# Padding the tiles of xT and the slots of the split weights so that they stand at different offsets within 512 bytes

## The reference, cut to what matters

```python
qkv = h @ w_qkv                                   # 2048 x 6144
x = x + y @ w_o                                   # 2048 x 2048
x = x + (silu(conv(h @ w_gate)) * (h @ w_up)) @ w_down        # width 5632
...
c_q, c_kv, k_rope, q_d, k_d, v_d, q_idx, k_idx, w_idx = split(h @ w_in)
x = x + concat([mla(...), dsa(...)]) @ w_out
x = x + cross_attention(h, mem)
x = x + square(relu(h @ w_up)) @ w_down           # width 8192
return rmsnorm(x, g_final)
```

## Time and profile before

| | |
|---|---|
| median of 2 runs | 2344.15 us (2344.14 to 2344.16) |
| span of the profiled execution | 2342.6 us |
| PE busy | 2329.2 us, 12126 matmuls |
| weight loads (PEld) busy | 1990.3 us |
| VectorE busy | 1569.7 us |
| ScalarE busy | 1232.0 us |
| DMA | 436.20 MB, 186 GB/s on average |

### The profile page before, as it was taken

One profiled execution on the slowest core, in us unless ns is written; L12 is line 12 of the kernel. 1 busy time (PEld: TensorE's weight loads), 2 busy tenths in 40 slices (PEclk: granted clock), 3 DMA queues, 4 the chain that ended last, 5 costly groups with the idle time before them and its releaser, 6 DMA issues.

```text
span 2342.6 us, 31399 instructions
## 1 busy us (share of the span) xinstructions
PE 2329.2 (99%) x12126; PEld 1990.3 (85%) x12126; DVE 1569.7 (67%) x2464; ACT 1232.0 (53%) x1877; POOL 4.3 (0%) x11
## 2 busy tenths in 40 slices
PE   9999999999999999999999999999999999999998
PEld 7888888888888888888888888888888888888887
DVE  7797877777777557755668556666766556556555
ACT  6566666555555445544656555656445345345343
POOL 0000000000000000000000000000000000000000
PEclk9999999999999999999999999999999999999999
DMA  8555455556555556565564545654555665655664
GB/s 313 171 162 179 137 168 165 178 183 204 182 180 206 191 178 204 181 219 189 165 205 156 177 152 161 226 181 159 192 188 181 206 189 180 204 192 182 216 194 153
DMA packets 119300, 436.20 MB, mean 186 GB/s; under 512 B 13392, under 2 KB 13648, under 8 KB 118128
## 3 DMA queue, kind: packets, MB, share of 16 engines
q1 hardware_dynamic: 117792, 426.13, 55.3%
q0 software_dynamic: 928, 7.47, 0.9%
q10 hardware_dynamic: 432, 0.60, 0.1%
HBM read 432.05 MB, written 2.10 MB: 185 GB/s over the span
## 4 chain that ended last, share of the span: by engine, by line
PE 98%; DVE 1%; DMA 1%; ACT 0%; issue 0%; SPq 0%
PE bank L511 30%; PE bank L493 16%; PE bank L495 16%; PE bank L494 16%; PE bank L525 16%; PE bank L575 1%; DMA x<-in_x 0%; PE bank L793 0%; PE bank L805 0%; PE bank L617 0%; PE bank L603 0%; PE bank L639 0%; DVE lo_w L1463 0%; PE bank L752 0%; PE bank L776 0%; PE bank L713 0%
## 5 line engine op out<-in xcount | busy, mean ns | idle before, releaser
L1463 DVE TENSOR_TENSOR lo_w<-raw_w,hi_w 128x1024 fp32r<-128x1024 f32 x804 | 965.0, 1218 | 537.9 <-ACT hi_w L994 536.6
L994 ACT ACTIVATE hi_w<-raw_w 128x1024 fp32r<-128x1024 f32 x804 | 833.9, 1053 | 581.8 <-PE bank L495 398.9
L511 PE MATMUL bank<-xT,hi_w 128*128 128x512 f32 x3008 | 720.9, 391 | 1.5 <-ACT hi_w L994 1.5
L511 PEld LDWEIGHTS bank<-xT,hi_w 128*128 128x128 f32 x3008 | 552.3, 188 | 108.4 <-DVE xT L1648 1.9
L525 PEld LDWEIGHTS bank<-xT,lo_w 128*128 128x128 f32 x3008 | 387.5, 191 | 17.2 <-DVE lo_w L1463 1.8
L525 PE MATMUL bank<-xT,lo_w 128*128 128x256 f32 x3008 | 396.4, 283 | 1.4 <-DVE lo_w L1463 1.4
L493 PE MATMUL bank<-hi_w,act_hi 128*128 128x512 f32 x864 | 336.4, 389 | 0.0
L495 PE MATMUL bank<-hi_w,act_lo 128*128 128x512 f32 x864 | 336.1, 389 | 0.0
L494 PE MATMUL bank<-lo_w,act_hi 128*128 128x512 f32 x864 | 336.1, 389 | 0.0
L493 PE MATMUL bank<-hi_w,xT 128*128 128x512 f32 (+1 forms) x672 | 265.4, 395 | 0.0
L495 PE MATMUL bank<-hi_w,xT 128*128 128x512 f32 (+1 forms) x672 | 260.9, 388 | 0.0
(11 more groups left out here) (339 smaller groups left out, 1565.3 us busy)
## 6 DMA issues: line engine op xcount, KB each, us to landing
raw_w<-in_w_up SPq DMA_DIRECT2D x216, 512.0 KB, 4.2
raw_w<-in_w_down SPq DMA_DIRECT2D x216, 512.0 KB, 3.5
raw_w<-in_w_gate SPq DMA_DIRECT2D x88, 512.0 KB, 4.2
raw_w<-in_w_in SPq DMA_DIRECT2D x72, 512.0 KB, 3.7
raw_w<-in_w_qk SPq DMA_DIRECT2D x64, 512.0 KB, 4.1
raw_w<-in_w_v SPq DMA_DIRECT2D x32, 512.0 KB, 3.6
raw_w<-in_w_o SPq DMA_DIRECT2D x32, 512.0 KB, 3.5
raw_w<-in_w_out SPq DMA_DIRECT2D x32, 512.0 KB, 3.6
```

The costliest lines, as they stand in the source:

```text
L511: last = e.matmul(pair[c][:, :], hi_w[:, slot, at:at + P], both[:, kt].rearrange("p h t -> p (h t)"), start=(kt == 0), stop=(kt == g.kts - ...
L994: e.activation(hi_w[:, u % SPLIT_SLOTS, 0:unit_cols[u]], raw_w[:, u % RAW_SLOTS, 0:unit_cols[u]], ACT.Copy).then_inc(s["w_hi"], 1)
L1463: e.tensor_tensor(lo, raw_w[:, u % RAW_SLOTS, 0:unit_cols[u]], hi.bitcast(F32), ALU.subtract).then_inc(s["w_lo"], 1)
```

## The change

The slots of `hi_w` grow by 64 floats (256 bytes) and stand 4352 bytes apart, those of `lo_w` by 8 floats (32 bytes) and stand 4128 bytes apart. Each tile of `xT` grows by 4 floats (16 bytes), and tiles stand 2064 bytes apart; its view leaves the padding out, so that all accesses name the same elements as before. The tensor `pad` grows from 240 to 400 floats, so that what is declared behind it stands 2048 bytes further than before. No instruction is added, removed or moved.

```diff
--- before.py
+++ after.py
@@ -35,6 +35,7 @@
 RAW_SLOTS = 4
 SPLIT_SLOTS = 4
 WARM = 12
+HI_PAD, LO_PAD, X_PAD = 64, 8, 4
 Q_SCALE = HD ** -0.5
 
 EXPS = "natural_log_exp_and_others"
@@ -214,14 +215,14 @@
                     sbuf(prefix + "pT", [P, 2, TOK], F32, scope), sbuf(prefix + "small", [P, 4, 8], F32, scope))
 
         raw_w = sbuf("raw_w", [P, RAW_SLOTS, UNIT])
-        hi_w = sbuf("hi_w", [P, SPLIT_SLOTS, UNIT], F32R)
-        lo_w = sbuf("lo_w", [P, SPLIT_SLOTS, UNIT], F32R)
+        hi_w = sbuf("hi_w", [P, SPLIT_SLOTS, UNIT + HI_PAD], F32R)
+        lo_w = sbuf("lo_w", [P, SPLIT_SLOTS, UNIT + LO_PAD], F32R)
         x = sbuf("x", [P, TT, D])
-        xT = sbuf("xT", [P, DK, 2, TOK], F32R)
+        xT = sbuf("xT", [P, DK, 2 * TOK + X_PAD], F32R)[:, :, 0:2 * TOK].rearrange("p k (h t) -> p k h t", h=2)
         consts = sbuf("consts", [P, n_const])
         gains = sbuf("gains", [P, n_gain])
         stats = sbuf("stats", [P, 192])
-        sbuf("pad", [P, 240])
+        sbuf("pad", [P, 400])
         banks = [ctx.enter_context(nc.psum_tensor(f"bank{i}", [P, 512], F32)) for i in range(8)]
         s = {name: ctx.enter_context(nc.semaphore(name)) for name in SEMAPHORES}
```

## The result

The changed kernel takes **2369.12 us** at the median (2369.07 to 2369.18, 2 runs), against 2344.15: a ratio of 1.0107 with a 95% interval of 1.0078 to 1.0137. It is 25 us slower than before, where 11 us were forecast (2355): 14 us over the forecast, inside the range, and a difference of 1.1%.

The account below looks back on a forecast made before the run. TensorE's matmul spacing was taken as the bound. 7968 wide matmuls at 1.35 ns gave 11 us, narrow ones and splits zero; 2342.6 + 11 = 2353.6, plus 1.6 us around the span: forecast 2355 us, range 2300 to 2396.

Parts of the forecast that it names:

- The bound: TensorE's matmul spacing sets the time; no input, other engine or transfer does, PE's longest wait being 1.9 us in total.
- the 1.35 ns for each wide matmul: Forecast cost of differing offsets for each of 7968 matmuls of 512 columns, middle of 0 and 2.7 ns: 11 us.
- the tail's 64-byte groups: Matmuls of the 400-wide tail product standing 64 bytes off the common offset, read at 180.0 ns: no price for the offset.
- the straight line: Line through spacings of 226.7 ns at 512 columns and 119.4 at 256, giving 179.8 ns at 400.
- Rival B: Changing offsets keep high_products and product from settling: 5.5 ns per wide, 2 per narrow matmul, 50 us, 2394; chance 0.16.
- the small forecast: Small shifts, 2335 to 2370 us, down-projection spacings within 224 to 230 ns; chance 0.58 with A and D.
- The narrow products: The 3120 matmuls of 256 columns, spaced at 119.4 ns; the forecast took zero change for them.
- v_m against v_d: Value products 128 bytes off the moving a_pT against those at the same offset: 2 to 3 ns dearer when offsets differ.
- the settled state: Spacing of 226.7 ns that a stream of 512-column matmuls settles into; being out of it costs 5.5 ns.
- A: Nothing moves, offsets don't matter: 2344 us; counted with the forecast and D at 0.58.
- C: The 13 ns over the columns are two reads clashing at one offset: 139 us gain in full, half 2274; chance 0.12.
- D: A slower split comes through in the attention part: 2355 to 2365 us; within the 0.58 of forecast with A.

Follow-up runs that it names:

- The maps: Original kernel, each group's hi_w (first run) or lo_w (second) starting 16 x (n mod 32) bytes into its slot: 2373.75 and 2363.99 us against 2344.29.

## Why the prediction was near, and where it was wrong

*The bound.* Right: no wait, engine or transfer entered. Counts, clock, splits and transposes stayed, as the page and the groups after show.

*The term of the sum that was mis-sized* is the 1.35 ns for each wide matmul. All kinds of wide products together rose by 29.7 us over 7968, which is **3.7 ns**. I took the middle between 0 and 2.7 because the tail's 64-byte groups lay on the straight line. That reading was rounding in part: by the start times of the whole tail these groups take 181.5 ns for each matmul, 1.7 over the line, and those at the common offset 183.7. And the same 64 bytes cost a 512-column stream in a down projection 6.6 ns (233.3). The maps show that this was the weak row: the price goes up and down from offset to offset (228.8 to 233.8 for wide products), so one offset at one width says nothing of the others. Rival B's price, 5.5 ns from the stream after an attention matmul, was nearer, and its mechanism was half right: with changing offsets the stream doesn't reach 226.7 any more. But B's cause, the change from one matmul to the next, isn't needed: one constant shift of 16 bytes does it. By my own mark (a down projection outside of 224 to 230) the small forecast was wrong; 231.3 said so, and with 3.70 to 3.72 us for sixteen wide ones it stands at B's signs. That the time came within 14 us is luck in part: the wide ones alone would have given 2374, and the narrow ones, which I had at zero, took 5 us back.

*The narrow products* I priced at zero, B at +2 ns. They fell by 1.6 ns, 5 us in all. The sign was not foreseen, and the row under it (v_m against v_d) turned out not to show the offset. The error behind it: I took the settled state for the fastest one. For 256 columns at offset 0 it is 120, and most unsettled sequences are below that.

*The rivals.* A, that offsets can't matter, is refuted by a control and a test: 512 bytes more pitch move nothing, 16 bytes of shift move 7 us with no other edit. The rule in the Trainium skill, "TensorE: Matmul & The Clock Gate", Part 2, is that two independent read ports keep the loading of weights from taking read bandwidth from the running matmul. What the prediction drew from it, that offsets can't matter, doesn't hold for these streams: a shift of the weights of the narrow products alone moves their spacing between 116.6 and 120.2 ns. Whether the two reads meet at a port, or something else about a start address changes the pace, no run here shows. C, that the 13 ns over the columns are a clash that other offsets remove, did not come for the wide ones: in no map is a mean under 226.7. For the narrow ones it is half true: 12.7 ns fall to 6.6 where they settle at 113.3. D did not occur.

*What stays open:* the cause of the price in the chip. The runs show that offsets set the spacing; they don't show what has the period of 256 bytes, or why a pair of offsets has the sequence that it has. Offsets between multiples of 16 bytes were not tried, nor whether a shift of xT also repeats after 256 bytes, nor whether the wide products have an offset pair, with xT moved too, that settles under 226.7.

## What to carry to other kernels

This was seen with float32r products that load new weights for every matmul; other forms were not tried. When TensorE is the bound and its matmuls follow each other without waits, read the spacing from start times by kind and look for its repeating sequence. Where tensors begin within 256 bytes then is a tuning knob of some per cent of a matmul in either direction; spreading offsets is no remedy by itself, and a common offset can be the best place. Put a different offset into each group of one run and read the map from the trace, instead of timing one layout after the other.

## What was not expected of the hardware

The spacing of weight load and matmul pairs is a sequence without noise: the same offsets, entered in the same state, give the same sequence to a nanosecond in group after group. Before the change the sixteen narrow spacings of a run add up to 1912 or 1913 ns in all but the few runs that hold a wait, though ScalarE is busy for 14% of one such run and throughout another. It has more than one place to settle for one kind of matmul: 226.7 and 233.3 ns for 512 columns at offsets of 0 and 64 bytes, 113.3 and 120.0 for 256. At 2.4 GHz (granted clock 1.00), with one column a cycle, these are 13.3, 20.0, 6.7 and 13.3 ns over the columns, all multiples of 6.7 ns, or 16 cycles by this estimate. Before the change a stream of wide ones spends up to ten matmuls at 224 to 240 ns before it settles, so what stands in front of a stream has a price in it.
